# Half of the output projection's attention rows moved between the last levels of a triangular inverse, with attention's end ahead of them and other PSUM banks

## The reference

```python
z = _rmsnorm(h, mix_pre_g[l]) @ w_in[l]
y_att = _attention_group(z[..., :ATT_IN], cos, sin, attn_out_g[l])
y_rwkv = _rwkv7_group(z[..., ATT_IN:], ...)
mix = jnp.concatenate([y_att, y_rwkv], axis=-1) @ w_out[l]
h = h + _rmsnorm(mix, mix_post_g[l])

def _rwkv7_step(state, inp):
    r, w, k, v, kk, kka = inp
    sa = jnp.einsum('dbhvk,dbhk->dbhv', state, kk)
    state = state * w[..., None, :] - sa[..., :, None] * kka[..., None, :] + v[..., :, None] * k[..., None, :]
    y = jnp.einsum('dbhvk,dbhk->dbhv', state, r)
    return state, y
```

## Time and profile before

| | us |
|---|---|
| median of 3 runs | 1143.54 (1142.17 to 1143.81) |
| profiled execution | 1142.37 |
| its span | 1140.6 |
| PE busy | 1123.6 of the span |
| POOL busy | 917.1 |
| ACT busy | 633.9 |
| DVE busy | 542.2 |

### The profile page before, as it was taken

How to read it: one execution, slowest core, us unless ns; L and a number is a source line. 1 busy time by engine, 2 the same in 40 slices (tenths; PEclk the granted TensorE clock), 3 DMA queues, 4 the chain that set the end, 5 groups by cost and what they waited for, 6 DMA issues and landing times.

```text
span 1140.6 us, 24340 instructions
## 1 busy us (share of the span) xinstructions
PE 1123.6 (99%) x10090; PEld 1048.1 (92%) x10090; DVE 542.2 (48%) x1006; ACT 633.9 (56%) x1024; POOL 917.1 (80%) x709
## 2 busy tenths in 40 slices
PE   9999999999999999999999999999999799999998
PEld 9998999999998999999999999999988679999997
DVE  5542575642653223222644333467986466233333
ACT  6666675447644654444744444588664437444443
POOL 6997667875996999989799999698785036999994
PEclk9999999999999999999999999999999999999999
DMA  7655445555565665565556565565610035556563
GB/s 287 194 168 183 129 131 166 204 164 151 185 222 184 211 190 187 189 185 185 166 185 187 186 186 187 193 201 165 199 55 23 4 113 186 186 186 187 188 188 101
DMA packets 54302, 193.50 MB, mean 170 GB/s; under 512 B 6448, under 2 KB 7344, under 8 KB 53808
## 3 DMA queue, kind: packets, MB, share of 16 engines
q1 hardware_dynamic: 52464, 185.41, 51.2%
q10 hardware_dynamic: 1728, 6.53, 1.5%
HBM read 188.77 MB, written 1.05 MB: 166 GB/s over the span
## 4 chain that ended last, share of the span: by engine, by line
PE 95%; DVE 2%; POOL 1%; issue 1%; ACT 1%; DMA 0%; DVEq 0%; POOLq 0%; ACTq 0%
PE product L635 19%; PE product L637 19%; PE product L636 19%; PE bank L765 8%; PE bank L767 7%; PE bank L766 7%; PE product L1382 2%; PE bank L1337 1%; PE bank L1331 1%; PE product L864 1%; PE product L1331 1%; PE product L793 1%; PE product L865 1%; PE product L866 1%; PE bank L822 1%
## 5 line engine op out<-in xcount | busy, mean ns | idle before, releaser
L583 POOL TENSOR_TENSOR weight_lo<-raw_ring,weight_hi 128x512 fp32r<-128x512 f32 x684 | 892.1, 1337 | 191.3 <-ACT weight_hi L2772 177.7
L2772 ACT ACTIVATE weight_hi<-raw_ring 128x1024 fp32r<-128x1024 f32 x338 | 356.7, 1059 | 362.6 <-DMA raw_ring<-in_ffn_gu 108.6
L635 PE MATMUL product<-operand_B_hi,weight_hi 128*128 128x256 f32 x1104 | 312.0, 283 | 0.2 <-POOL weight_lo L583 0.2
L637 PE MATMUL product<-operand_B_hi,weight_lo 128*128 128x256 f32 x1104 | 310.9, 282 | 0.0
L636 PE MATMUL product<-operand_B_lo,weight_hi 128*128 128x256 f32 x1104 | 310.5, 281 | 0.0
L635 PEld LDWEIGHTS product<-operand_B_hi,weight_hi 128*128 128x128 f32 x1104 | 207.8, 188 | 3.3 <-POOL weight_lo L583 0.4
L636 PEld LDWEIGHTS product<-operand_B_lo,weight_hi 128*128 128x128 f32 x1104 | 207.9, 188 | 3.1
L637 PEld LDWEIGHTS product<-operand_B_hi,weight_lo 128*128 128x128 f32 x1104 | 207.8, 188 | 0.0
L635 PE MATMUL product<-operand_A_hi,weight_hi 128*128 128x256 f32 x712 | 203.8, 286 | 0.1
L636 PE MATMUL product<-operand_A_lo,weight_hi 128*128 128x256 f32 x712 | 200.4, 282 | 0.0
L637 PE MATMUL product<-operand_A_hi,weight_lo 128*128 128x256 f32 x712 | 200.4, 281 | 0.0
(11 more groups left out here) (436 smaller groups left out, 1538.6 us busy)
## 6 DMA issues: line engine op xcount, KB each, us to landing
raw_ring<-in_w_in SPq DMA_DIRECT2D x95, 512.0 KB, 3.6
raw_ring<-in_ffn_gu SPq DMA_DIRECT2D x88, 512.0 KB, 3.6
raw_ring<-in_ffn_down SPq DMA_DIRECT2D x44, 512.0 KB, 3.5
raw_ring<-in_w_mlp_up SPq DMA_DIRECT2D x32, 512.0 KB, 3.6
raw_ring<-in_w_mlp_down SPq DMA_DIRECT2D x32, 512.0 KB, 3.5
raw_ring<-in_w_out SPq DMA_DIRECT2D x14, 512.0 KB, 3.7
raw_ring<-in_w_gmlp_v SPq DMA_DIRECT2D x8, 512.0 KB, 3.5
raw_ring<-in_w_branch_c SPq DMA_DIRECT2D x8, 512.0 KB, 3.5
```

The costliest lines, as they stand in the source:

```text
L583: last = k.nc.gpsimd.tensor_tensor(k.wlo[:, slot, part], k.raw[:, slot, part], k.whi[:, slot, part].bitcast(F32), ALU.subtract)
L635: mm(ps, w_hi, op.hi[:, b, :], start=b == 0, stop=False)
L637: return mm(ps, w_lo, op.hi[:, b, :], start=False, stop=b == blocks - 1)
L2772: k.nc.scalar.activation(k.whi[:, slot, 0:w], k.raw[:, slot, 0:w], ACT.Copy).then_inc(k.s["hi_ready"], 1)
```

## The change

- PE: rows 0, 2, 4 and 6 (the first token half) leave the place behind `solve(2)` and go between the levels from `left_and_both(2, 3, 3, 2)` on, mostly one pair at a time. Rows 1, 3, 5 and 7 stay behind the levels, the first two of them split around other steps. `attention_by_feature` goes ahead of `left_and_both(3, 2, 2, 2)`. `values_first(1)` and `state_behind(1)` become `from_state(1)`.
- DVE and ACT: `attention_out(7)`, the sums, the norm and the lows on DVE and squares, root and highs on ACT come earlier. ACT loads the square root's table by a one-column activation between `probabilities(6)` and `probabilities(7)`.
- Banks: rows of the first token half fill banks 0 and 1, so chunks 2 and 3 use banks 2 and 3 and slots 0 and 1 for their levels, and `chunk_products(3, 0)`, `keys_by_token(2)` and attention's transposes use banks 0 and 1. State 0 goes to the chain's bank.
- The order of ACT behind the levels and SP's order are as before.

```diff
-    k.state_banks = (k.slots[1], k.chain_bank, k.slots[1])
-    k.left_banks, k.both_banks = (k.bank[1], k.slots[0]), (k.bank[0], k.bank[3])
+    k.state_banks = (k.chain_bank, k.chain_bank, k.slots[1])
+    k.left_banks = ((k.bank[1], k.slots[0]), (k.slots[1], k.slots[0]))
+    k.both_banks = ((k.bank[0], k.bank[3]), (k.bank[2], k.bank[3]))
-    k.turn_bank = [k.bank[2], k.slots[1]]
+    k.turn_bank = [k.bank[0], k.bank[1]]
...
     left_and_both(2, 2, 3, 1)
-    values_first(1)
+    attention_by_feature()
     left_and_both(3, 2, 2, 2)
-    state_behind(1)
+    from_state(1)
     left_and_both(2, 3, 3, 2)
+    half_row(0)
     solve(1)
     left_and_both(3, 3, 2, 3)
+    half_row(2, slice(0, 1))
     to_state(1)
     left_and_both(2, 4, 3, 3)
-    attention_by_feature()
+    half_row(2, slice(1, 2))
     left_and_both(3, 4, 2, 4)
+    half_row(4, slice(0, 1))
     from_state(2)
     left_and_both(2, 5, 3, 4)
+    half_row(4, slice(1, 2))
     left_and_both(3, 5, 2, 5)
+    half_row(6, slice(0, 1))
     last_both(3)
+    half_row(6, slice(1, 2))
     solve(2)
-    half_row(0)
-    half_row(1)
     state_first(2)
     solution_behind(2)
     values_first(3)
-    half_row(2)
+    half_row(1, slice(0, 1))
     state_behind(3)
-    half_row(3)
+    half_row(1, slice(1, 2))
     solve(3)
-    half_row(4, slice(0, 1))
+    half_row(3, slice(0, 1))
+    last_outputs(3)
     feature_major(0)
-    last_outputs(3)
-    half_row(4, slice(1, 2))
-    for n in range(5, 2 * AB):
-        half_row(n)
-
+    half_row(3, slice(1, 2))
+    half_row(5)
+    half_row(7)
     inner_tokens(4)
     inner_tokens(5)
     feature_major(1)
...
     first_turned(2)
-    chunk_products(3, 0, SPARE_BANKS)
+    attention_out(7)
+    chunk_products(3, 0, LANES[0])
     left_alone(2, 1)
-    attention_out(7)
+    attention_sums()
     first_turned(3)
     for level in range(1, 5):
         between_levels(3, level, 2, level)
         if level == 1:
-            attention_sums()
+            attention_norm()
+        elif level == 2:
+            attention_lows()
         between_levels(2, level + 1, 3, level)
         if level == 1:
             new_state(0)
-        elif level == 2:
-            attention_norm()
...
     left_alone(3, 5)
-    attention_lows()
     new_state(2)
...
-    rwkv_values(0, 0)
     outputs(3)
     v.wait_ge(s["y_taken"], 4)
     y_norm(1, 0)
+    rwkv_values(0, 0)
...
     probabilities(6)
+    f(sm[:, 144:145], k.eps[:, 0:1], ACT.Sqrt)
     probabilities(7)
+    attention_squares()
     right_side(0)
...
     solution(0)
-    attention_squares()
+    attention_root()
     inverse(2, 1)
     outputs(0)
     inverse(3, 1)
-    attention_root()
+    attention_highs()
     inverse(2, 2)
```

More of the change, by code:

```diff
@@ L1330, in left_product @@
         n = (k.nf if level in FLIPPED else k.nt)[j % 2]
-        return mm(column(k.left_banks[u // 4], u)[rows], n[rows, u, :], k.tc[j % 2][rows, u, :], start=True, stop=True)
+        return mm(column(k.left_banks[j // 2][u // 4], u)[rows], n[rows, u, :], k.tc[j % 2][rows, u, :], start=True, stop=True)
     def both_product(bank, j, level, u, d):
@@ L1353, in last_both @@
             for d in range(2):
-                last = both_product(k.both_banks[1], j, 5, u, d)
+                last = both_product(k.both_banks[j // 2][1], j, 5, u, d)
         last.then_inc(s["tt_mm"], 2)
@@ L1367, in left_and_both @@
                 for d in range(2):
-                    last_both = both_product(k.both_banks[part], other, at_level, u, d)
+                    last_both = both_product(k.both_banks[j // 2][part], other, at_level, u, d)
             last_left.then_inc(s["u_mm"], 1)
@@ L1515, in state_first @@
         state_of_values, _, _, state_kept = state_parts(j)
-        pe.wait_ge(s["op_ready"], k.made["y_mix"].base + AB)
+        pe.wait_ge(s["u_ev"], nth(3, 5))
         for u in range(8):
@@ L1643, in half_row @@
         if n == 0:
-            pe.wait_ge(s["tt_ev"], nth(2, 5))
-            pe.wait_ge(s["u_ev"], nth(3, 5))
+            pe.wait_ge(s["op_ready"], k.made["y_mix"].base + AB)
         elif n == 1:
             pe.wait_ge(s["tt_ev"], nth(3, 5))
-            pe.wait_ge(s["op_ready"], k.made["y_mix"].base + AB)
         j = n // 2
@@ L2600, in level_left @@
         four = slice(4 * part, 4 * part + 4)
-        nv.tensor_tensor(k.uc[j % 2][:, four], units(k.left_banks[part])[:, four],
+        nv.tensor_tensor(k.uc[j % 2][:, four], units(k.left_banks[j // 2][part])[:, four],
                          k.levels[:, level:level + 1, :].to_broadcast([P, 4, RC]), ALU.mult).then_inc(s["u_ev"], 1)
@@ L2606, in turned @@
         v.wait_ge(s["tt_mm"], nth(j, level, part))
-        nv.transpose(part_of(flat(k.tc[j % 2]), part), part_of(k.both_banks[part], part)).then_inc(s["t_ev"], 1)
+        nv.transpose(part_of(flat(k.tc[j % 2]), part), part_of(k.both_banks[j // 2][part], part)).then_inc(s["t_ev"], 1)
     def between_levels(j, level, other, at_level):
@@ L3298, in attention_squares @@
         act.wait_ge(s["o_ev"], ATT_HEADS)
-        f(k.att_p.rearrange("p a b -> p (a b)"), k.att_o.rearrange("p a b -> p (a b)"), ACT.Square).then_inc(s["o_squares"], 1)
+        f(k.att_p.rearrange("p a b -> p (a b)"), k.att_o.rearrange("p a b -> p (a b)"), ACT.Square).then_inc(s["o_sq"], 1)
     def outputs(j):
@@ L3339, in inverse @@
             four = slice(4 * part, 4 * part + 4)
-            f(k.ttc[j][:, four], units(k.both_banks[part])[:, four], ACT.Copy).then_inc(s["tt_ev"], 1)
+            f(k.ttc[j][:, four], units(k.both_banks[j // 2][part])[:, four], ACT.Copy).then_inc(s["tt_ev"], 1)
     def last_inverse(j):
         act.wait_ge(s["tt_mm"], nth(j, 5))
-        f(k.ttc[j], units(k.both_banks[1]), ACT.Copy).then_inc(s["tt_ev"], 2)
+        f(k.ttc[j], units(k.both_banks[j // 2][1]), ACT.Copy).then_inc(s["tt_ev"], 2)
     def keys_by_token(j, banks):
@@ L3410, in scalar_program @@
     inverse(2, 3)
+    outputs(1)
     inverse(3, 3)
-    outputs(1)
     inverse(2, 4)
-    attention_highs()
     right_side(2)
```

15 lines of the change are left out of this document (6 added, 9 removed).

## The result

The changed kernel took 1152.59 us (median of 4 executions, 1150.03 to 1153.70), the kernel before 1143.67 beside it: a ratio of 1.0077, with an interval of 1.0058 to 1.0096. The forecast was +4.9 us with a range up to 1151.8; it came out at +8.9. The direction was right and the size was not. The traced execution is the quickest of the four, 1150.03 with a span of 1148.2, so +7.7 on the traced execution of before. The 2.5 us between it and the other three are a part of the answer.

A forecast was written before the change was run, and what follows sets the result against it. PE was taken to bound the kernel, with holes in the levels mostly waits for code. Start and levels +0.3, tail +3.1 and clock +1.5 summed to +4.9 us, predicting 1148.4 us, range 1144.6 to 1151.8.

The forecast's parts named there:

- the levels' net of +0.9: Between the levels: pieces add 7.0 us, less 1.0 for moved transposes and 5.1 of holes filled, giving +0.9 us.
- the 0 for the clock behind the second idle: Ahead of feature_major(1): PE idles 2.7 us, under 3, so no slow clock is charged; bounds 0 to 1.6 us.
- Start of the levels: Ahead of from_state(0): PE's wait of 1.24 us goes, first_turned(3) is late next; gain 0.6 us, between 0 and 1.24.
- is made up in the next: In the levels: idle in a code block without a piece is recovered in the following block, whose code comes no later.
- credit of 1.0 for the transposes: In the later levels: moving attention_by_feature's transposes to the first levels saves 1.0 us and costs nothing there.
- Tail: From solve(2) to feature_major(1): idles of 6.2 and 2.7 us from late weight tiles; 28.9 against 25.75 us, +3.1.
- Clock behind the first idle: From solve(3) on: the clock falls in the 6.2 us idle and the slow restart costs +1.5 us, bounds 0 to 1.6.
- rival (d): Ahead of feature_major(1): the second idle drops the clock too, or y_norm(1) is later still; +1.6 us, 1150.0; chance 15%.
- rival (a): In the levels: pieces are not absorbed and add up; up to 5.1 us more, 1153.5; chance 10%.
- main case: Whole kernel: start and levels, tail and first restart of the clock together cost +4.9 us; chance 35%.

## Why the prediction was wrong in size

Two terms of the sum failed: the levels' net of +0.9, which measured +3.2, and the 0 for the clock behind the second idle, which measured 2.5 in most executions. The others held.

**Start of the levels: right.** The wait of 1.24 ahead of `from_state(0)` went, and one of 0.74 for `first_turned(3)` (L2594) came ahead of the first level, the step that the prediction had named as next. From a common point (the first transpose of `keys_by_token(0)`, around 833) to the first level the eleven traces of the changed order take 42.7 to 43.3 us (mean 43.0), the two of before 43.3 and 43.8: 0.5 gained, 0.6 forecast.

**Levels: mechanism right, size wrong.** The step that failed is "net 7.0 - 1.0 - 5.1 = +0.9"; it measured +4.0 in the traced pair and +3.2 between the means (35.0 against 31.8). With the gain of 0.5 at the start this still lies inside the bounds of -0.3 to +5.4. Two things in it were wrong. The holes were summed over the stretch and all counted as filled, because what a block without a piece idles "is made up in the next". Of the 5.07 us behind 889.99, the changed kernel kept 2.3: 1.26 in the block from 900.80, which has no piece, and 0.58 and 0.38 at two other borders. And three pieces stand behind 904.54, where there was only 0.84 to fill: 6.66 us there against 4.45 before. The credit of 1.0 for the transposes that leave the later levels failed as well: the work was taken out of a block that waits for code at its end, and no time given back for it shows (32.22 with them moved and no pieces, 31.43 and 32.25 before). Of the 2.3 between the forecast's +0.9 and the means' +3.2 the holes account for about 1.0 (4.1 of the pieces hidden, not 5.1) and the credit for the rest. Making up was seen, in the second trace of the changed kernel, whose levels took 33.7: it can happen but could not be counted on.

**Tail: right, and nearly to the digit.** `solve(3)` 15.29 us behind `solve(2)`, forecast 15.3; idle 5.96, forecast 6.2. The second idle 3.42, forecast 2.7: from `outer_squares` to the end of `y_norm(1)` it took 3.22 instead of 2.78, because DVE's last step there ran 1.14 us instead of 0.69 while POOL was at work on weights. The thirteen traces agree on this: the step takes 1.13 or 1.14 in the four in which POOL works beside it, 0.69 in the seven in which POOL rests, and 0.82 and 0.88 in the two in which POOL's work ends inside it. No run moved POOL's work alone. Another 0.2 is the landing, 4.73 from SP's issue to the high part where 4.53 was taken. The runs with the high parts moved and with tile 0 released early show the cause by two separate ways.

**Clock behind the first idle: right.** +1.5 forecast, 1.7 measured: 12.35 us from `solve(3)` to `feature_major(1)` without the idle, 10.63 in the run with tile 6's high part late, in which the clock did not fall there. Its size owes something to chance: a slow stretch of 3.2 us was taken, and it lasted 4.0.

**Clock behind the second idle: wrong.** The text took 0, "for PE idles less than 3 us there", and kept 1.6 for rival (d). It idles 3.1 to 3.4, the clock falls in seven of nine executions (so far as times tell), and it costs 2.5 when it does, because 5.4 to 5.8 us of dense matmuls go at half the clock behind it. The reason given for the 0 was weak by the prediction's own rows: at the kernel's end the clock had fallen 2 to 3 us behind the last matmul, and 2.7 lies within that. In the traces it fell 2.0 to 2.1 us into this idle, so with an idle of the forecast length it could have fallen too. The rule of the Trainium skill that the prediction weighed ("TensorE: Matmul & The Clock Gate", section "Part 1: The HAM clock gate (the "warmup" mystery)") had pointed that way, and three of the four traces with this idle agree (a granted clock of 0.50 in idles of 3.12, 3.30 and 3.44 us); in the fourth, of 3.42, it stayed at 1.00. Rival (d) together with a good part of rival (a) is what happened; the range had room for one of them, not for both, since each was priced against a main case without the other.

Summed with these sizes: -0.5 + 3.2 + 5.2 + 2.5 = 10.4 in an execution with two falls of the clock. The nine executions have a median of 1152.5, some 9.6 above before's 1142.9 in the comparisons with the most executions.

## What to carry to other kernels

When work is moved on the engine that bounds a kernel, follow the last use of every buffer that it releases: the DMA behind that release, and what stands behind the wait for it on an in-order engine, can cost more than the move gains. Holes of an instruction stream are not a sum to be filled. Count them block by block, and expect only a part of what is put in to be hidden: here some 4 of 7.0 us. One piece to a block was the best version measured; that its placement is what made it so is not shown. And a stall of some microseconds on PE is to be priced with the slow matmuls behind it: here 1.7 and 2.5 us for idles of 6.0 and 3.4.

## What the runs showed of the hardware

- The granted clock fell from 1.00 to 0.50 (2.4 to 1.2 GHz) in PE's idles of 6.0 to 6.3 us in all four traces that have one, 3.1 to 4.0 us behind the last matmul. In idles of 3.1 to 3.4 us it fell in three of four traces, 2.0 to 2.1 us behind the last matmul; what decides there stays open. It was back at 1.00 some 4.0 to 5.8 us after PE's first matmul.
- Code arrives in blocks of 126 matmuls with their weight loads, and the fetch has its own scatter: the same block without a piece was 3.3 to 4.2 us long, once 5.1, and the whole of the levels 31.4 to 32.3 in two executions of one kernel and 33.7 to 35.4 in two of the other. A single trace can't tell less than a microsecond there.
- With large matmuls between the small ones holes at the borders can vanish. From about 890 to 901 us the kernels without pieces wait for code twice (0.7 to 1.3 us each); with the changed kernel's pieces six of seven traces show no such wait there, and the seventh one of 0.38. The holes near 881, 885 and 889, ahead of the pieces, mostly stay, and so does the one near 904 in the six traces that have no piece in front of it (0.9 to 1.5 us).
- A DVE product over 128x512 elements (the last step of `y_norm(1)`) took 0.69 us in the seven traces with POOL at rest and 1.13 or 1.14 in the four with POOL at work on the weights; in the other two POOL ended inside it and it took 0.82 and 0.88. A DVE reduction over as many elements took 0.69 with POOL at work as well.
